# First products by token tile and half unit, memory turned inside the first feed-forward part, parameters loaded in pieces, S5 preparation in two parts

## The reference

```
for l in range(2):
    h = swiglu(x, w_gate[l,0], w_up[l,0], w_down[l,0])      # 1024 -> 2816 -> 1024
    x = layer_norm(ALPHA*x + 0.5*h)
    x = layer_norm(ALPHA*x + hybrid_mix(x))                 # DiffAttn | mLSTM | S5, then w_out
    x = layer_norm(ALPHA*x + memory_cross_attention(x, mem))  # kv = mem @ wkv
    h = swiglu(x, w_gate[l,1], w_up[l,1], w_down[l,1])
    x = layer_norm(ALPHA*x + 0.5*h)
```

## Time and profile before

| | |
|---|---|
| Time, median of 3 runs | 1317.14 us (1315.62 to 1317.58) |
| Profiled execution, its own time | 1315.97 us |
| Span in its trace | 1313.9 us |
| Instructions | 16451 |
| DMA | 219.46 MB, mean 167 GB/s |

### The profile page before, as it was taken

One profiled execution on the slowest core, in us unless ns is written; L12 is line 12 of the kernel. 1 busy time (PEld: TensorE's weight loads), 2 busy tenths in 40 slices (PEclk: granted clock), 3 DMA queues, 4 the chain that ended last, 5 costly groups with the idle time before them and its releaser, 6 DMA issues.

```text
span 1313.9 us, 16451 instructions
## 1 busy us (share of the span) xinstructions
PE 1265.5 (96%) x6896; PEld 1084.2 (83%) x6896; DVE 772.0 (59%) x1011; ACT 589.9 (45%) x670; POOL 161.1 (12%) x161
## 2 busy tenths in 40 slices
PE   6999999999999999999999999999998999999997
PEld 5788888897889888888887888889887897788885
DVE  4578646585537565454565687565756646655543
ACT  5443544445524435433444444545345344533441
POOL 1008800000001000000001068200001200000000
PEclk8999999999999999999999999999999999999999
DMA  7755545531254365555557555545322543655550
GB/s 272 244 186 191 190 163 166 174 105 66 101 182 144 124 224 185 181 185 189 191 184 245 191 174 182 191 160 167 107 81 72 198 147 128 197 189 192 192 186 38
DMA packets 160041, 219.46 MB, mean 167 GB/s; under 512 B 6848, under 2 KB 136000, under 8 KB 159968
## 3 DMA queue, kind: packets, MB, share of 16 engines
q1 hardware_dynamic: 156544, 205.61, 47.0%
q0 software_dynamic: 3152, 11.76, 2.7%
q10 hardware_dynamic: 272, 1.05, 0.2%
HBM read 217.34 MB, written 1.05 MB: 166 GB/s over the span
## 4 chain that ended last, share of the span: by engine, by line
PE 87%; DVE 5%; DMA 4%; ACT 3%; issue 2%; SPq 0%; POOL 0%; POOLq 0%; DVEq 0%; ACTq 0%
PE PS L485 26%; PE PS L487 26%; PE PS L486 26%; DMA RAW<-in_ffn_w_up 2%; PE PS L516 1%; DVE WL L1478 1%; ACT WH L1091 1%; PE PS L553 1%; PE PS L1005 1%; PE PS L1029 1%; PE PS L703 1%; DMA RAW<-in_w_out 1%; DMA RAW<-in_w_in 0%; PE PS L801 0%; PE PS L759 0%
## 5 line engine op out<-in xcount | busy, mean ns | idle before, releaser
L1478 DVE TENSOR_TENSOR WL<-RAW,WH 128x2048 fp32r<-128x2048 f32 (+1 forms) x198 | 447.9, 2266 | 262.7 <-ACT WH L1091 262.5
L1091 ACT ACTIVATE WH<-RAW 128x2048 fp32r<-128x2048 f32 (+1 forms) x198 | 370.3, 1880 | 175.0 <-DMA RAW<-in_ffn_w_up 124.5
L485 PE MATMUL PS<-WH,XH 128*128 128x512 f32 x768 | 307.1, 400 | 8.7 <-DVE XL L1478 7.5
L487 PE MATMUL PS<-WH,XL 128*128 128x512 f32 x768 | 300.4, 391 | 0.0
L486 PE MATMUL PS<-WL,XH 128*128 128x512 f32 x768 | 300.3, 391 | 0.0
L485 PEld LDWEIGHTS PS<-WH,XH 128*128 128x128 f32 x768 | 144.9, 189 | 40.6 <-issue 8.0
L487 PEld LDWEIGHTS PS<-WH,XL 128*128 128x128 f32 x768 | 144.7, 188 | 30.8
L486 PEld LDWEIGHTS PS<-WL,XH 128*128 128x128 f32 x768 | 145.2, 189 | 28.6 <-issue 0.5
L485 PE MATMUL PS<-WH,HH 128*128 128x512 f32 x352 | 138.5, 394 | 4.7 <-issue 4.7
L487 PE MATMUL PS<-WH,HL 128*128 128x512 f32 x352 | 137.8, 391 | 0.0
L486 PE MATMUL PS<-WL,HH 128*128 128x512 f32 x352 | 137.6, 391 | 0.0
(11 more groups left out here) (318 smaller groups left out, 1787.1 us busy)
## 6 DMA issues: line engine op xcount, KB each, us to landing
RAW<-in_ffn_w_gate SPq DMA_DIRECT2D x88, 512.0 KB, 3.7
RAW<-in_ffn_w_up SPq DMA_DIRECT2D x88, 512.0 KB, 4.7
RAW<-in_ffn_w_down SPq DMA_DIRECT2D x88, 512.0 KB, 4.3
RAW<-in_w_in SPq DMA_DIRECT2D x44, 512.0 KB, 4.2
RAW<-in_xattn_wkv SPq DMA_DIRECT2D x32, 512.0 KB, 4.4
RAW<-in_xattn_wq SPq DMA_DIRECT2D x16, 512.0 KB, 4.0
RAW<-in_w_out SPq DMA_DIRECT2D x12, 512.0 KB, 4.4
RAW<-in_xattn_wo SPq DMA_DIRECT2D x12, 512.0 KB, 3.9
```

The costliest lines, as they stand in the source:

```text
L485: nc.tensor.matmul(out_ap, sh, mh, start=first, stop=False)
L487: return nc.tensor.matmul(out_ap, sl, mh, start=False, stop=last)
L1091: return nc.scalar.activation(dst, src, ACT.Copy)
L1478: return v.tensor_tensor(dst, full, hi.bitcast(F32), ALU.subtract)
```

## The change

Nothing is computed otherwise, apart from 16 small products of the S5 tables that become two large ones. The edits:

- SP loads tile 0 of x first, then unit 0 in four transfers of half the size (`load_first`), with an event of its own for the first two chunks; the identity matrix goes over ACT's queue; tile 1 of x follows unit 1, and the memory follows unit 4.
- PE turns x tile 0 first and begins the products of unit 0 as soon as the first half of x tile 0 and the first half of the unit are split. ACT and DVE split unit 0 in two halves, with the halves of x around them.
- The memory is turned inside the first feed-forward part, 4 transposes after the down product of blocks 1 to 4 (`turn_memory`), split by ACT and DVE after their steps (`memory_turned`).
- POOL loads `PAR` and `PDL` when unit 2 has landed, the other parameters when unit 5 has, the remaining constants after unit 7 and `LNGB` after unit 9. Layer 1's parameters are loaded during layer 0, after the mixer's norm, right behind a load of `LNGB`.
- `prepare_rest` ends with `lam_ready`; its second half is `prepare_last`, two steps later. `tables` stages 1 and 2 and the sine on ACT come one step later. `scale_c` starts at `lam_ready` and waits for `cur_ready` in its middle.

```diff
         @block.sync
-            sp.dma_start(ident, const[:, K_ID:K_ID + P]).then_inc(const_in.sem, 16)
-            sp.dma_start(X[:, :, :], x_in.rearrange("b (t p) d -> p (b t) d", p=P)).then_inc(x_loaded.sem, 16)
+            x_v = x_in.rearrange("b (t p) d -> p (b t) d", p=P)
+            sp.dma_start(X[:, 0, :], x_v[:, 0, :]).then_inc(x_loaded[0].sem, 16)
...
+            def load_first():
+                r = raw(0).rearrange("p (c g n) -> p c g n", c=4, g=2)
+                for i, event in enumerate((first_in, raw_loaded[0])):
+                    cs = slice(2 * i, 2 * i + 2)
+                    sp.dma_start(r[:, cs, 0, :], wg_v[0, :, cs, 0:FB]).then_inc(event.sem, 16)
+                    sp.dma_start(r[:, cs, 1, :], wu_v[0, :, cs, 0:FB]).then_inc(event.sem, 16)
...
                 load_gu(l, s, 1, 0, 1)
+                if l == 0 and s == 0:
+                    sp.dma_start(X[:, 1, :], x_v[:, 1, :]).then_inc(x_loaded[1].sem, 16)
                 for j in range(BLOCKS - 1):
...
                     load_down(l, s, 4 + 3 * j, j)
+                    if l == 0 and s == 0 and j == 0:
+                        sp.dma_start(MEMX[:, :, :], mem_in.rearrange("b (t p) d -> p (b t) d", p=P)).then_inc(mem_loaded.sem, 16)
...
         @block.tensor
                 if l == 0 and s == 0:
                     turn_x(0, 0, 0)
-                turned(l, n, 0)
-                unit_ready(b)
-                gate_up_tile(b, 0, 0)
+                    pe.wait_ge(xT_lo.sem, xT_lo.at(0, 1))
+                    pe.wait_ge(first_lo.sem, 1)
+                    gate_up_tile(b, 0, 0, 0, 2)
+                    unit_ready(b)
+                    gate_up_tile(b, 0, 0, 2, 4)
...
                     rows_product(b + 4 + 3 * j, [0, 1], HH, HL, False, False)
+                    if l == 0 and s == 0 and j <= 4:
+                        turn_memory(j - 1)
...
+            def turn_memory(g):
+                t, half = g // 2, g % 2
+                if g == 0:
+                    pe.wait_ge(mem_loaded.sem, 16)
+                else:
+                    pe.wait_ge(mem_lo.sem, g)
+                for i in range(4):
+                    c = 4 * half + i
+                    mm = nc.tensor.transpose(PS[:, 7, i * P:i * P + P], MEMX[:, t, c * P:c * P + P], ident)
+                mm.then_inc(mem_psum.sem, 1)
...
         @block.scalar
-            act.dma_start(MEMX[:, :, :], mem_in.rearrange("b (t p) d -> p (b t) d", p=P)).then_inc(mem_loaded.sem, 16)
-            for i in range(4):
-                act.wait_ge(xT_psum.sem, i + 1)
...
-            split()
-            turned(0, 0, 0)
+            act.dma_start(ident, const[:, K_ID:K_ID + P]).then_inc(const_in.sem, 16)
+            turned_half(0, 0, 0, 0)
+            act.wait_ge(first_in.sem, 32)
+            copy(WH[0][:, 0:1024], RAW[0][:, 0:1024]).then_inc(first_hi.sem, 1)
+            act.wait_ge(raw_loaded[0].sem, 32)
+            copy(WH[0][:, 1024:2048], RAW[0][:, 1024:2048]).then_inc(split_hi.sem, 1)
+            turned_half(0, 0, 0, 1)
...
         @block.vector
                 v.tensor_tensor(CUR[:, R_RAD:R_RAD + 8], th, th, ALU.mult)
                 dve.wait_ge(prep_sin.sem, prep_sin.at(l, 1))
+                v.tensor_tensor(ni, w, SW[:, 0:8], ALU.mult)
+                v.tensor_tensor(CUR[:, R_LRE:R_LRE + 8], w, SW[:, 8:16], ALU.mult).then_inc(lam_ready.sem, 1)
+
+            def prepare_last(l):
...
         @block.gpsimd
-                pool.wait_ge(unit_used.sem, UNIT[l, "F0", 0] + 1)
-                pool.dma_start(PAR[:, :], par[l, :, 0:P_END]).then_inc(param_in.sem, 16)
...
+            pool.wait_ge(raw_loaded[2].sem, 32)
+            load_params(0)
+            pool.wait_ge(raw_loaded[2].sem, 64)
+            pool.dma_start(kst[:, P:K_END], const[:, P:K_END]).then_inc(const_rest.sem, 16)
+            pool.wait_ge(raw_loaded[4].sem, 64)
...
                 pool.wait_ge(x_ready.sem, x_ready.at(l, 4))
                 load_gb(l, 2)
+                if l + 1 < DEPTH:
+                    load_params(l + 1)
```

More of the change, by code:

```diff
@@ L545, in turn_x @@
             def turn_x(l, n, t):
-                pe.wait_ge(x_ready.sem, x_ready.at(l, TT * (n - 1) + t + 1))
+                if l == 0 and n == 0:
+                    pe.wait_ge(x_loaded[t].sem, 16)
+                else:
+                    pe.wait_ge(x_ready.sem, x_ready.at(l, TT * (n - 1) + t + 1))
                 for half in range(2):
@@ L567, in ffn @@
                     turn_x(0, 0, 0)
-                turned(l, n, 0)
-                unit_ready(b)
-                gate_up_tile(b, 0, 0)
+                    pe.wait_ge(xT_lo.sem, xT_lo.at(0, 1))
[3 more added lines that the diff above has]
+                    gate_up_tile(b, 0, 0, 2, 4)
+                else:
+                    turned(l, n, 0)
+                    unit_ready(b)
+                    gate_up_tile(b, 0, 0)
                 bare = s == 1 and not FILL["ffn2", l]
@@ L685, in s5_turn @@
                 pe.wait_ge(lb_ready.sem, lb_ready.at(l, k + 1))
+                if l == 0 and k == 0:
+                    pe.wait_ge(mem_lo.sem, 4)
                 if k > 0:
@@ L1140, in ffn @@
                 step(1, False)
+                if l == 0 and s == 0:
+                    memory_turned(0)
                 if s == 0:
@@ L1610, in ffn @@
                 step(2, False)
+                if l == 0 and s == 0:
+                    memory_turned(1)
                 if s == 0:
@@ L1614, in ffn @@
                     step(j, False)
-                    if s == 0 and j < 6:
-                        tables(l, j - 3)
+                    if l == 0 and s == 0 and j <= 4:
+                        memory_turned(j - 1)
+                    if s == 0 and j == 3:
+                        tables(l, 0)
+                    if s == 0 and j == 4:
+                        prepare_last(l)
+                    if s == 0 and j == 5:
+                        tables(l, 1)
+                    if s == 0 and j == 6:
+                        tables(l, 2)
                 step(BLOCKS - 2, True)
@@ L2042, in _ @@
             v.memset(ones_c[:, :], 1.0)
-            dve.wait_ge(x_loaded.sem, 16)
-            dve.sem_inc(x_ready.sem, TT)
-            for i in range(4):
-                t, half = i // 2, i % 2
-                dve.wait_ge(xT_hi.sem, i + 1)
-                low(ML[:, 4 * half:4 * half + 4, t * P:t * P + P], PS[:, i, :].rearrange("p (c n) -> p c n", c=4),
-                    MH[:, 4 * half:4 * half + 4, t * P:t * P + P]).then_inc(xT_lo.sem, 1)
-            split()
-            turned(0, 0, 0)
+            assert next(units) == 0
+            turned_half(0, 0, 0, 0)
+            dve.wait_ge(first_hi.sem, 1)
+            low(WL[0][:, 0:1024], RAW[0][:, 0:1024], WH[0][:, 0:1024]).then_inc(first_lo.sem, 1)
+            dve.wait_ge(split_hi.sem, 1)
+            low(WL[0][:, 1024:2048], RAW[0][:, 1024:2048], WH[0][:, 1024:2048]).then_inc(split_lo.sem, 1)
+            turned_half(0, 0, 0, 1)
             split()
```

121 lines of the change are left out of this document (74 added, 47 removed).

## The result

| | before | changed |
|---|---|---|
| Time, median | 1316.87 us (4 runs) | 1301.13 us (4 runs, 1299.99 to 1304.04) |
| Ratio | | 0.9885, 95% interval 0.9873 to 0.9897 |
| Profiled execution | 1315.97 us, span 1313.9 | 1304.04 us, span 1302.2 |

The changed kernel is faster, by 15.7 us where 12.0 was forecast. Yet the profiled execution took what the forecast gave for it, 1304.0. The traces have to explain both.

A forecast was written before the change was run, and what follows sets the result against it. TensorE, busy 96% of the span, was the bound, leaving 48 idle us and slow-clock stretches to gain. 8.4 + 2.24 + 1.7 - 2.0 - 1.75 + 1.1 + 2.3 = 12.0 us, so 1305.1 us, 8 in 10 from 1302.3 to 1309.8.

The forecast's parts named there:

- The first product: Start of layer 0: TensorE's first product at 8.8 us instead of 17.2, between 6.7 and 10.9.
- The start: Start of layer 0: halved pieces and splits let the products begin earlier, a gain of 8.4 us.
- The new waits in blocks 0 and 1: First feed-forward part, layer 0: PAR and PDL delay units 3 and 4; TensorE idles 1.1 and 0.9 us, 2.0 lost.
- The old hole and its slow stretch: Layer 0, at 42.60 us: the wait for hidden block 0's low part goes, 2.24 us, and 8 slow products, 1.7.
- The memory: First feed-forward part, layer 0: 16 transposes now stand between products, 1.75 us lost, upper bound 2.6.
- The preparation and layer 1's parameters: Preparation in two parts gains 0.6 us in layer 0, 0.5 in layer 1; earlier parameters gain 2.3 in layer 1.
- the median lies 1.17 above it: Last step of the sum: the profiled execution, forecast at 1304.0 us, lies 1.17 under the median, so 1305.1.
- (b): Rival, layer 0: weights lag the earlier start, units 3 and 4 bind 2 us more, clock falls; 1308.8 us, chance 0.22.
- (c): Rival, start: small pieces are slower, three more issues on SP put everything behind back by 1.4 us; 1307.5, chance 0.08.
- (d): Rival, layer 1: it keeps its waits, gain 9.7 us, so 1307.4; chance 0.07.
- (e): Rival, layer 0: slower than before because unit 5, behind the memory on SP's queue, is late; 1319 us, chance 0.01.
- PEclk falls again after 22 us: Sign that the prediction is wrong: TensorE's clock falls again after the one slow stretch at the start.

The follow-up runs named there:

- The split alone: Changed kernel with layer 1's parameters loaded at its own start again, when its unit 0 has been used: median 1305.57 us, ratio to before 0.9921.
- The parameters alone: Changed kernel with the S5 preparation in one part again, its second half before HL of block 3: median 1308.34 us, ratio to before 0.9937.

## Why the prediction was right and where it failed

**The first product** was forecast at 8.8 and stands at 8.9 to 9.2; unit 5 at 28.2, landed at 28.3. The start gained 7.5 of 8.4: 0.4 for the first product, the rest because 12 products and not 10 ran at the slow clock. By the Trainium skill, "TensorE: Matmul & The Clock Gate", Part 1, the number of slow matmuls at a start varies from run to run. The traces agree: tile 1 of x came 4.3 to 5.3 us after the first product in the four traces of before, and 4.7 to 5.3 in the three of the changed kernel.

On the means of four and three traces the start gained 8.1 us, so this term was near. The rest of the first part gained 3.0, where 0.8 was forecast.

**The new waits in blocks 0 and 1** are the term that failed most: 2.0 us forecast, 0.3 to 0.7 measured in all (0.27; 0.40 and 0.30; 0.32). The step was to let the bytes of PAR and PDL flow from the moment of their issue, in front of the rest of unit 3, which so landed at 19.4. POOL's queue moved nothing before 19.5 to 19.75 us in the three traces of the changed kernel, and unit 3 landed at 18.5. So ACT ended silu 0 at 22.1 instead of 23.0 and HB was done at 23.1, while TensorE came to it only at 23.9, 1.1 later than forecast: no first wait. Unit 4 did land where the forecast had it (22.35 against 22.3), but ACT was free for it 0.6 us earlier, and 0.3 us is left of the second wait. By the Trainium skill, "DMA: Bandwidth & Descriptors", Queues, rings and completion order, the engines take turns between queues with work. The last piece of unit 4 agrees (9.6 us to landing beside PAR's packets, 8.4 without them); unit 3 says nothing on it, because POOL's queue had moved no packet when it landed.

**The old hole and its slow stretch** were priced at 2.24 and 1.7, 8 slow products. The traces of before show the wait at 2.24, 2.88, 2.51 and 2.36 and 8, 13, 8 and 8 slow products behind it, so the one trace was the lowest draw.

**The memory** came at its price. **The preparation and layer 1's parameters**: I took 0.5 and 2.3 us from separate rows, 2.8 in all; both together gave 3.7, on 198.1 us. The idle times were read as the whole cost. The rows say why they are not: an idle time is counted from the modelled end of the last product, 0.39 us after its start, while products follow each other at 0.23, and the first product after a wait holds up its follower by nearly 0.1 (89.25 to 89.56 above). That is some 0.25 for each wait, 0.8 for three, and 2.9 and 0.8 make 3.7. How the gain is shared between the two edits is less sure. The split alone gave 0.4. The parameters alone stand at 198.7, a loss of 0.6, but in that run 1.6 us of the wait and the 1.7 of the clock come from POOL's earlier start; without them I estimate 195.4, a gain of 2.7. No run has the parameters alone with POOL as before.

**From the trace to the median.** The sum over the changed stages was 12.0 and comes out at 14.8 (11.1 and 3.7) against the mean of four traces. Of the difference of 2.8, about 1.5 is the new waits, 0.9 the idle times of layer 1, and 0.7 the hole, its slow products and the wait at block 3 in layer 0, all three at or near their lowest in the one trace; the start takes 0.3 back. The last step, "the median lies 1.17 above it", failed too: the profiled execution is a draw, and the offset of one kernel does not carry over. That of before was 1.2 us under its median (1317.15 over 26 executions), that of the changed kernel 2.5 above its own (1301.50 over 12). The mixers alone ranged over 171.1 to 174.6 and 147.3 to 150.0 in 14 traces, with the same program in them. With the mixers taken as equal, 14.8 and 0.2 outside the span (1.8 instead of 2.0) make 15.0, near the medians' 15.6. The seven traces themselves differ by 12.9 in their mean spans (1314.2 and 1301.3): the traced executions of before stood on average 1.0 under its median, those of the changed kernel 1.6 above. Whether the mixers run longer on average in the changed kernel, where their stretches stand elsewhere in time, stays open; three traces and four can't tell.

**The rest.** `prepare_last` before HL of block 5 brought no wait: its cover of 3 us held. Of the rivals, (b), (c), (d) and (e) did not occur: PEclk did not fall between 22 us and the mixer, the small pieces landed as early as the large ones, layer 1 has no wait left in its first feed-forward part, and unit 5 was in time. The sign "PEclk falls again after 22 us" did appear, in both mixers; it was drawn too wide, since the kernel before has such falls there too (PEclk 0.96 over 320 to 400 us).

## What to carry to other kernels

Cut two traces at the same instructions and compare stage by stage before you explain a total: stages that the change doesn't touch show at once what is luck. When you undo one edit to price it, look whether the other edits still act on it: here POOL's earlier start lengthened the very operations that were put back. Add to an idle time what its row leaves out. And take a size that hangs on a wait or on the clock from several executions, not one.

## What the hardware showed unexpectedly

- A stretch at the slow clock cost nothing where TensorE waited for another engine anyway (7.39 us from AT to SDA with and without it), and up to half its length elsewhere (2.7 of 6.8 us in mixer 1, 1.7 of 3.4 behind a wait for HL). The same mixer took 171.1 to 174.6 us in layer 0 and 147.3 to 150.0 in layer 1.
- PEclk is given as 1.00 for 8 to 14 us in the changed kernel, where every product takes 0.43 us. In these first microseconds the pace shows the clock, and the record doesn't.
- A transfer of 508 KB issued on POOL's queue at 15.8 us moved its first packet after 19.75 (in the kernel before, issued at 28.8, after 31.3). It left one issued at 9.0 untouched, which had landed by then, and delayed one issued at 12.7 by 1.2 us.
- DVE's operations of 128x8 that took 0.17 us alone took up to 0.6 while POOL multiplied 128x256 beside them.
